# An encoder trunk on one core: x loaded ahead of the modulation weights, the recurrent gates' blocks loaded later, and the first transposed x evicted by channel block

## The reference

```python
cs = jax.nn.silu(c)
mod = cs @ mod_w[0] + mod_b[0]                  # (1, 6144)
sh1, sc1, g1, sh2, sc2, g2 = jnp.split(mod, 6, axis=-1)
h = rmsnorm(x, norm_mix_g[0]) * (1 + sc1) + sh1
z = h @ w_in                                    # (512, 1024) @ (1024, 2560)
...
xr = depthwise_conv(b_in, conv_b_w, 1) + conv_b_b
r = sigmoid(einsum('bshi,hij->bshj', xh, wa) + ba)   # 8 heads of 64 channels, block diagonal
i = sigmoid(einsum('bshi,hij->bshj', xh, wx) + bx)
```

## Time and profile before

| | |
|---|---|
| three runs | 1544.82, 1678.39, 1680.1 us |
| median | 1678.39 us |
| profiled execution, span | 1678.9 us |
| PE busy | 1494.5 us, 89% |
| DVE, ACT, POOL busy | 923.6, 586.6, 91.4 us |
| mean granted clock of PE | 0.857 of full |
| moved by DMA | 353.18 MB, mean 210 GB/s |

### The profile page before, as it was taken

One profiled execution on the slowest core, in us unless ns is written; L12 is line 12 of the kernel. 1 busy time (PEld: TensorE's weight loads), 2 busy tenths in 40 slices (PEclk: granted clock), 3 DMA queues, 4 the chain that ended last, 5 costly groups with the idle time before them and its releaser, 6 DMA issues.

```text
span 1678.9 us, 15037 instructions
## 1 busy us (share of the span) xinstructions
PE 1494.5 (89%) x5233; PEld 977.5 (58%) x5233; DVE 923.6 (55%) x1344; ACT 586.6 (35%) x790; POOL 91.4 (5%) x133
## 2 busy tenths in 40 slices
PE   2899999399999998499989999999956999999892
PEld 2445455266667764288866666666535677766540
DVE  6588824667777771566642222222356777777304
ACT  1265002355555550322122222221234555555201
POOL 4000000100000000200000000000001000000001
PEclk9999999599999999699995555555977999999996
DMA  8946680369999987456370000000033999999644
GB/s 279 365 161 211 200 314 38 124 236 363 374 360 368 385 317 287 163 176 238 103 284 27 0 1 0 0 1 1 25 138 126 365 371 370 369 364 347 238 163 163
DMA packets 79747, 353.18 MB, mean 210 GB/s; under 512 B 12824, under 2 KB 13008, under 8 KB 70736
## 3 DMA queue, kind: packets, MB, share of 16 engines
q1 hardware_dynamic: 64704, 326.65, 52.6%
q0 software_dynamic: 8352, 20.46, 3.4%
q10 hardware_dynamic: 6640, 5.42, 1.0%
HBM read 334.15 MB, written 28.31 MB: 216 GB/s over the span
## 4 chain that ended last, share of the span: by engine, by line
PE 87%; DVE 6%; ACT 2%; DMA 2%; issue 2%; ACTq 1%; POOL 0%; DVEq 0%; POOLq 0%; SPq 0%
PE ps L1533 21%; PE ps L1544 14%; PE ps L1446 9%; PE ps L1632 8%; PE ps L1662 7%; PE ps L1474 7%; PE ps L1673 6%; PE ps L1687 4%; PE ps L1524 3%; PE ps L1519 2%; PE ps L1420 2%; PE ps L1538 1%; PE ps L1487 1%; PE ps L1456 1%; ACTq L636 1%
## 5 line engine op out<-in xcount | busy, mean ns | idle before, releaser
L1544 PE MATMUL ps<-slab_ring,scratch 128*128 128x512 f32 x560 | 246.5, 593 | 3.4 <-ACT scratch L783 2.1
L1533 PE MATMUL ps<-slab_ring_r,gate_rows_r 128*128 128x512 f32 x512 | 202.2, 395 | 0.0
L1544 PEld LDWEIGHTS ps<-slab_ring,scratch 128*128 128x128 f32 x560 | 105.8, 190 | 124.2 <-issue 117.3
L1229 DVE TENSOR_TENSOR slab_ring_r<-slab_ring,h_t_r 128x2048 fp32r<-128x2048 f32 x64 | 143.8, 2288 | 22.7 <-ACT h_t_r L735 22.7
L1364 DVE CUSTOM_DVE_ANT_0 mod_ring<-ps,log_count 128x512 f32<-128x512 f32 x64 | 44.2, 691 | 197.0 <-PE ps L1662 197.0
L1446 PE MATMUL ps<-h_t,slab_ring 128*128 128x512 f32 x320 | 146.1, 617 | 0.0
L1662 PE MATMUL ps<-h_t,scratch 64*128 64x512 f32 x128 | 127.4, 1106 | 0.9 <-DVE h_t L1355 0.9
L1632 PE MATMUL ps<-slab_ring_r 128*128 128x512 f32 x384 | 123.6, 404 | 1.7 <-DVE h_t_r L902 1.7
L817 ACT ACTIVATE mod_ring<-mod_ring,neg_max 128x512 f32<-128x512 f32 x64 | 46.2, 722 | 217.9 <-DVE neg_max L1365 217.9
L1533 PE MATMUL ps<-h_t_r,gate_rows_r 128*128 128x512 f32 x256 | 106.3, 415 | 14.7 <-DVE scratch_r L1223 14.7
L735 ACT ACTIVATE h_t_r<-slab_ring 128x2048 fp32r<-128x2048 f32 x64 | 118.4, 1901 | 0.2 <-issue 0.2
(11 more groups left out here) (286 smaller groups left out, 2200.2 us busy)
## 6 DMA issues: line engine op xcount, KB each, us to landing
slab_ring<-in_expert_w_gate_dram SPq DMA_DIRECT2D x35, 2048.0 KB, 10.3
slab_ring<-in_expert_w_up_dram SPq DMA_DIRECT2D x35, 2048.0 KB, 10.2
slab_ring<-in_expert_w_down_dram SPq DMA_DIRECT2D x35, 2048.0 KB, 10.4
mod_ring<-in_mod_w_dram SPq DMA_DIRECT2D x64, 512.0 KB, 4.7
y_rows<-scratch SPq DMA_DIRECT2D x35, 512.0 KB, 10.8
slab_ring<-in_mod_w_dram SPq DMA_DIRECT2D x32, 512.0 KB, 4.7
slab_ring<-in_w_qkv_dram SPq DMA_DIRECT2D x6, 2048.0 KB, 11.9
slab_ring<-in_w_in_ab_dram SPq DMA_DIRECT2D x5, 2048.0 KB, 19.3
```

Source lines behind the costliest of these rows:

```text
L1229: tt_(rest, w, top.bitcast(F32), ALU.subtract).then_inc(low_ready[c], 1)
L1533: ins = pe.matmul(ps[:, bank, :], x, w, start=(kt == 0 and i == 0), stop=(kt == KT - 1 and i == 2))
L1544: ins = pe.matmul(ps[:, 5 + h, :], hidT[:, f, :], w[:, 2 * f + h, :], start=(f == 0), stop=(f == FT - 1))
```

## The change

SP issues the load of x ahead of the modulation slices. ACT no longer loads the gate blocks ahead of the norm but behind the evictions into h_t. DVE scales x between the slices of part 0, where it did so between those of part 1, and makes the mask after h_t. PE turns channel blocks 0 to 6 of all four token tiles before it reduces part 0, and block 7 after `mod_done` is 2. A channel block of all 512 tokens now lies in one PSUM bank, and an eviction takes a whole bank, 128x512: four on ACT (even blocks) and four on DVE (odd blocks). The wait for `bd_loaded` on PE stays where it was.

```diff
@@ SP
+        sp.dma_start(X[:, :, :], a["x"][0].rearrange("(t p) d -> p t d", p=P)).then_inc(x_loaded, 16)
         load_mod(0)
-        sp.dma_start(X[:, :, :], a["x"][0].rearrange("(t p) d -> p t d", p=P)).then_inc(x_loaded, 16)
         load_mod(1)
@@ ACT
-            act.wait_ge(bd_zeroed, 1)
-            for d in range(2):
-                for w, name in enumerate(("lru_wa", "lru_wx")):
-                    src = a[name][0, d].rearrange("(j two) i o -> two i j o", two=2)
-                    b0 = (d * 2 + w) * LRU_TILES
-                    for two in range(2):
-                        act.dma_start(BD[two * 64:(two + 1) * 64, b0:b0 + LRU_TILES, two * 64:(two + 1) * 64], src[two]).then_inc(bd_loaded, 16)
...
         act.wait_ge(mod_done, 2)
-        for t in range(TT):
-            take_ht(0, t)
+        for kt in range(0, KT, 2):
+            act.wait_ge(xn_turned, 3)
+            act.activation(HT[:, kt, :], ps[:, kt, :], ACT.Identity, bias=AB[:, 0, 1, kt:kt + 1], scale=AB[:, 0, 0, kt:kt + 1]).then_inc(ht_act, 1)
+        with nc.allow_non_contiguous_dma(reason="the heads' blocks, once"):
+            act.wait_ge(bd_zeroed, 1)
...
+                        act.dma_start(BD[two * 64:(two + 1) * 64, b0:b0 + LRU_TILES, two * 64:(two + 1) * 64], src[two]).then_inc(bd_loaded, 16)
         act.wait_ge(angle_ready, 1)
@@ DVE
-        mod_acc(0, 0, 8)
-
+        mod_acc(0, 0, 2)
+        for t in range(TT):
+            scale_x(0, t)
+            mod_acc(0, 2 + t, 1)
+        mod_acc(0, 6, 2)
+        mod_acc(1, 0, 5)
+        v.wait_ge(params_loaded, 16 * N_PARAMS)
+        mod_take(0)
+        mod_acc(1, 5, 3)
+        mod_take(1)
+        for kt in range(1, KT, 2):
+            v.wait_ge(xn_turned, 4 if kt == KT - 1 else 3)
+            ts(HT[:, kt, :], ps[:, kt, :], AB[:, 0, 0, kt:kt + 1], AB[:, 0, 1, kt:kt + 1], ALU.mult, ALU.add).then_inc(ht_dve, 1)
...
         v.sem_inc(mask_base, 1)
-
-        for t in range(TT):
-            scale_x(0, t)
-            mod_acc(1, 2 * t, 2)
-        v.wait_ge(params_loaded, 16 * N_PARAMS)
-        mod_take(0)
-        mod_take(1)
-        for t in range(TT):
-            take_ht(0, t)
@@ PE
         pe.wait_ge(consts_ready, 1)
+        for t in range(TT):
+            pe.wait_ge(xn_ready, t + 1)
+            for kt in range(KT - 1):
+                ins = pe.transpose(ps[:, kt, t * P:(t + 1) * P], xnorm[0][:, t, kt:D:KT], ident[:, :])
+            if t:
+                ins.then_inc(xn_turned, 1)
         mod_reduce(0)
-        for t in range(3):
-            turn_x(0, t)
         mod_reduce(1)
         pe.wait_ge(mod_done, 2)
-        turn_x(0, 3)
+        for t in range(TT):
+            ins = pe.transpose(ps[:, KT - 1, t * P:(t + 1) * P], xnorm[0][:, t, KT - 1:D:KT], ident[:, :])
+        ins.then_inc(xn_turned, 1)
```

More of the change, by code:

```diff
@@ L662, in _ @@
         act.wait_ge(mod_done, 2)
-        for t in range(TT):
-            take_ht(0, t)
+        for kt in range(0, KT, 2):
[3 more added lines that the diff above has]
+            act.wait_ge(bd_zeroed, 1)
+            for d in range(2):
+                for w, name in enumerate(("lru_wa", "lru_wx")):
+                    src = a[name][0, d].rearrange("(j two) i o -> two i j o", two=2)
+                    b0 = (d * 2 + w) * LRU_TILES
+                    for two in range(2):
+                        act.dma_start(BD[two * 64:(two + 1) * 64, b0:b0 + LRU_TILES, two * 64:(two + 1) * 64], src[two]).then_inc(bd_loaded, 16)
         act.wait_ge(angle_ready, 1)
```

## The result

| | runs | attention at 2.4 GHz | attention at 1.2 GHz |
|---|---|---|---|
| before, beside it | 4 | 1543.22, 1544.82 | 1678.39, 1680.1 |
| after | 4 | 1557.23, 1559.22 | 1693.49, 1694.45 |
| before, all 46 runs of this study | 46 | 21 runs, mean 1544.0 | 25 runs, mean 1681.0 |

The change makes the kernel slower. The runs of both kernels fall on two levels, 135 us apart, by the clock of the attention stage alone; so runs are compared within a level throughout. At the higher level the ratio is 1.0092, 95% interval 1.0049 to 1.0135: 14.2 us. At the lower level it is 14.7 us by these runs. Both kernels had two of four runs at each level, so the medians (1611.6 and 1626.4) lie in a gap where no run is. I had forecast 1682.6 for the lower level; it is 1694.0.

What follows compares the result with a forecast made beforehand. PE alone was taken to bound the kernel from the z start on; from 1678.4 us, z 10.0 us earlier without the gate blocks became 4.2 us later with their wait, giving 1682.6 us; range 1545 to 1692.

Steps and rivals of the forecast that it cites:

- z starts later because of the blocks: Input projection start: PE waits for the gate blocks until 59.0, so z starts 4.2 us later than before.
- ACT is free of its small loads at 11.97 (where L636 began), so the first square begins there: Norm start on ACT: first square of x at 11.97 instead of 24.75, 12.8 us earlier, first root at 14.8.
- I add 0.9 for those that are not: DVE's sums of modulation slices: 0.9 us added for slices not just in time, making the end 37.0 instead of 36.1.
- The blocks' term: Gate block loads beside the slabs: 12.4 us of transfer, 15.1 us from issue to landing, in at 59.0.
- Blocks from 43.9: ACT's queue: the eight gate block loads are issued behind its evictions, from 43.9 us.
- 1.5 us ahead of the first packet: Gate block loads: estimated delay of 1.5 us between the issue and the first packet.
- My lower bound: Gate blocks with hardly any other traffic: 6.1 us, in at 50.0, z 4.8 us early, time 1673.6 us.
- The eviction: Filling h_t by eight 128x512 evictions: ACT 2.5 us, DVE done at about 44.2, where it took 5.7 before.
- The mask work behind h_t costs nothing: Mask arithmetic moved behind h_t: 11 small DVE instructions at some 0.3 us lie under the first z tile, costing nothing.
- The z stage at 1.2 GHz for long: Fourth rival, z stage: idle PE keeps the low clock for five tiles, 34 us slower, 1717 us; chance 0.08.
- rival three: Attention stage at 2.4 GHz in the median run: 133.6 us less, 1549 us; chance 0.24.
- my highest price for the blocks: Upper bound of the gate blocks' transfer: 22.1 us, z at 68.7, 13.9 us late, time 1692.3 us.

Runs made afterwards that it cites:

- e1: Changed kernel with PE's wait for the gate blocks moved to the first gate product; 4.5 us (2.4 GHz) and 4.4 us (1.2 GHz) below the kernel before.
- e7: e1 with ACT's twelve small loads behind the squares of x; 10.8 us (2.4 GHz) and 7.7 us (1.2 GHz) below the kernel before.
- e6: e1 with eight places instead of four for the first sixteen modulation slices; 4.0 us (2.4 GHz) and 2.7 us (1.2 GHz) below the kernel before.
- e8: e1 with the edits of both e7 and e6; 1.9 us (2.4 GHz) and 2.5 us (1.2 GHz) below the kernel before.
- e9: e8 with three of the small loads put ahead of the squares; 7.0 us (2.4 GHz) and 8.7 us (1.2 GHz) below the kernel before.
- e10: Changed kernel with five of six slabs held until the gate blocks are in; 4.1 us (2.4 GHz) and 3.4 us (1.2 GHz) above the kernel before.
- h3: e7 with eight extra unread matmuls in attention steps 32 and 33; one run 1539.08 us, four from 1605.97 to 1608.76 us.
- e2: Changed kernel with the gate block loads back ahead of the squares; 0.5 us below (2.4 GHz) and 2.3 us above (1.2 GHz) the kernel before.
- e4: e1 with x loaded behind the first four modulation slices; 0.4 us below the kernel before at 1.2 GHz, no run at 2.4 GHz.

## Why the prediction was wrong

- **z starts later because of the blocks: right, and too small.** I had 4.2 us, it was 13.2. The mechanism (PE's wait for bd_loaded, one packet each for the two queues) was the measured one; e1 removes all of it. The sign was in the forecast; the size was off by 9.0 us, in the terms below.
- **The failed step: "ACT is free of its small loads at 11.97 (where L636 began), so the first square begins there".** It began at 15.45. I had moved x ahead of the slices and left the small loads' time as it was; but x and slices now kept queue 1 busy (98%) from 4.5 to 10.7 us, when the norm gains are issued, and one of them took 6.18 us, where before it took 1.60. The root followed at 18.30, where I had 14.8. That is 3.5 of the 6.8 us that mod_ab came late (48.2 for 41.4); e7 gets 4.4 back by moving these loads.
- **"I add 0.9 for those that are not": under-sized.** The slices' waits after the root are 1.44, 0.17, 0.30 and 1.94 us, 3.9 in sum, 3.0 more than I had. DVE's late root leaves the ring full and the DMA engines half idle (0.43 and 0.53), and the slices of part 1 then come one by one behind each other. e6, e8 and e9 show that more places bring nothing, since the small loads then come later.
- **The blocks' term.** "Blocks from 43.9" had them behind the evictions; ACT's queue issued the first beside them, at 48.26, when mod_ab was done, and not 2.5 us behind it: 2.5 us in the change's favour. "1.5 us ahead of the first packet" is what e10 shows on an empty queue; beside the full one it was 4.2. The transfer itself was well sized: 12.4 us forecast; at 1241 packets of queue 10 in 8 us (56 to 64) 2048 take 13.2. (A pair took 103 ns and not 97: the 14 ns for "a block packet" came from packets of 135 bytes in the mean, 0.05 MB in 371; the blocks' took 19.) What is left, 2.3, lies between and behind them, where I had 1.2. In all 19.7 for 15.1. (My lower bound, the blocks in at 50.0, left out the 2.7 us around the transfer; with them it is 52.7.)
- The sum: +6.8 (mod_ab) - 2.5 (issue beside the evictions) + 4.6 (19.7 for 15.1) = 8.9: the blocks landed at 67.95, where I had 59.0.
- **The eviction**: 2.8 forecast, 2.96 measured. Right, and it is the one part of the edit that gained. **The mask work behind h_t costs nothing**: right here, since its last piece on POOL ended at 65.8, inside the wait. **The z stage at 1.2 GHz for long**: fell; 80 matmuls took 36.02 us.
- **The attention.** The higher level was rival three with 0.24, one run in three; it is 42 in 95 for all kernels. With four runs the median could come out anywhere between the levels, and 1626.4 is inside my range without either side of it being tested. At the lower level the runs took 1694.0, above the 1692.3 of my highest price for the blocks: that bound was too low. It had z at 68.7 with the transfer at 22.1 us; z did start below that, at 68.0, but by another way, a late mod_ab and a transfer of 13.2.
- The Trainium skill (DMA: Bandwidth & Descriptors, Queues, rings and completion order) has an engine take a whole packet, typically 9 to 17 descriptors, from one queue before it changes to the next. I had let nine packets of the blocks go against one of the slabs', but the rule gives such a turn to both queues: then the counts can be equal as well, and neither the 2 to 3 us of my paragraph nor its 1672 follow from it. Nor do the equal counts (371 and 371, 625 and 624) speak against it. The starts of single packets say more. A packet of queue 1 takes 84 ns. I counted the pairs of starts on queue 1 by the time between them, in steps of 8 ns. While that queue is alone (48.3 to 52.3 us), the largest count below 120 ns is at 80 to 88 (1698 pairs): one packet behind another. Beside queue 10 (56 to 64 us) it is at 96 to 104 (1984, against 1516 at 80 to 88), the length of one packet of each queue. So the two queues took turns packet by packet here; nine or more of the profile's packets of one queue in a row would have kept the distance of 84. Whether the profile's packet is one descriptor of that page or a whole packet, the runs don't tell.

## What to carry to other kernels

A load that is moved to a later place is not only later: ask what the other queue holds at that place. A load of small packets beside a full queue pays the big queue's packet for each of its own, here 13 us for half a megabyte (7 us with the queue empty, issue and landing included), and a wait for it belongs at the first instruction that reads it. And when runs of one kernel fall on two levels, find what separates them before reading a difference of a per cent; here eight needless matmuls did more (135 us in half of the runs) than every ordering of the loads.

## What the runs showed that I had not expected

- **Two clocks for the same steps.** PE, busy through every window of the attention, was granted 0.50 for 280 us in some executions and 1.00 in others of the same kernel; a burst of four extra products (3.45 us, begun at the lower clock; 1.99 us at the higher) took it from 0.50 to 1.00 in the middle (h3), and all twenty runs that had two such bursts at the start were at the higher level. The Trainium skill (TensorE: Matmul & The Clock Gate, Part 1) says that activity releases the throttle; that more products raised the clock agrees, that a PE with busy 20.00 of 20.00 us stays at 0.50 does not. What a busy share of 100% leaves out of account here, the runs don't tell.
- **4.2 us to the first packet.** The first issue on ACT's queue beside SP's full one moved nothing for 4 us (772 packets of queue 1 and none of queue 10 at 48.3 to 52.3), on an empty one it took 1.5. Why, the runs don't tell.
- **An issue is not a fixed price.** The eight block loads took 12.7 us of ACT's queue before, 5.4 in e2, 7.4 after; the load of the norm gains 6.18 in the changed kernel and 1.50 in e7. The longest rows stand where the other queue is full, but that alone doesn't make them long: before, the same load of the norm gains took 1.60 beside a queue 1 that was busy throughout, and of the eight block loads after, with queue 1 at 98%, the first six took some 0.7 each and the last two 3.20 together. In five traces in which that load took over 5 us (after, e4, e6, e8, e9), ACT's queue had moved only 220 to 279 packets by the end of it, of the loads issued before. That an issue waits until ACT's own earlier packets have gone is what this suggests; no run tested it.
